# A routed-expert layer on one core: places behind the first two filled with heavy and light experts in turn

## The reference, cut to what matters

```python
logits = x2 @ w_router + b_router            # 256 x 32
top_vals, top_idx = lax.top_k(logits, 4)     # each token goes to 4 of 32 experts
# per expert e, for its tokens:
h = x2[tok] @ w_gu[e] + b_gu[e]              # w_gu[e]: 1024 x 2048, 8.39 MB
y = (clip(u) + 1) * (g * sigmoid(1.702 * g)) # g, u: the halves of h, clamped
out[tok] += gate * (y @ w_down[e] + b_down[e])   # w_down[e]: 1024 x 1024, 4.19 MB
```

## Time and profile before

| | us |
|---|---|
| median of three runs | 1148.16 |
| the profiled execution, its own time | 1148.07 |
| its span in the trace | 1146.2 |
| TensorE busy | 1062.1 |
| DMA queue of the weights, share of 16 engines' span | 91.2% |

### The profile page before, as it was taken

How to read it: one execution, slowest core, us unless ns; L and a number is a source line. 1 busy time by engine, 2 the same in 40 slices (tenths; PEclk the granted TensorE clock), 3 DMA queues, 4 the chain that set the end, 5 groups by cost and what they waited for, 6 DMA issues and landing times.

```text
span 1146.2 us, 20182 instructions
## 1 busy us (share of the span) xinstructions
PE 1062.1 (93%) x8033; PEld 465.3 (41%) x8035; DVE 443.7 (39%) x1311; ACT 153.0 (13%) x333; POOL 61.1 (5%) x39
## 2 busy tenths in 40 slices
PE   9999999998999669999976669999979989999997
PEld 8876559542333223333321113333323323333333
DVE  2767577582433113333321113333313323333324
ACT  2142111220111001111100001111101101111101
POOL 0503370000000000000000000000000000000000
PEclk9999999999999879999988879999989989999999
DMA  9965256989999999999999999999999999999995
GB/s 331 364 234 184 106 193 253 378 322 429 424 433 432 431 432 431 432 432 431 432 431 432 433 430 432 432 431 435 429 432 431 432 431 429 418 431 427 433 425 246
DMA packets 36105, 444.87 MB, mean 388 GB/s; under 512 B 3876, under 2 KB 5160, under 8 KB 21256
## 3 DMA queue, kind: packets, MB, share of 16 engines
q1 hardware_dynamic: 33320, 439.86, 91.2%
q10 hardware_dynamic: 2752, 4.54, 1.4%
HBM read 443.34 MB, written 1.05 MB: 388 GB/s over the span
## 4 chain that ended last, share of the span: by engine, by line
PE 73%; DMA 19%; DVE 3%; another core or an unknown queue 2%; ACT 1%; issue 1%; DVEq 0%; SPq 0%; POOL 0%; POOLq 0%
PE bank L1007 26%; DMA ring<-in_w_gu 14%; PE bank L1032 12%; PE bank L983 6%; PE bank L691 6%; DMA ring<-in_w_down 6%; PE bank L637 5%; PE bank L970 3%; PE bank L816 2%; PE bank L879 2%; PE bank L976 2%; PE bank L1014 1%; PE bank L1020 1%; PE bank L1025 1%; PE bank L1001 1%
## 5 line engine op out<-in xcount | busy, mean ns | idle before, releaser
L1007 PE MATMUL bank<-ring,wk 128*32 128x512 f32 x3072 | 373.3, 637 | 62.8 <-DMA ring<-in_w_gu 62.7
L1007 PEld LDWEIGHTS bank<-ring,wk 128*32 128x32 f32 x3072 | 104.1, 116 | 304.0 <-issue 265.7
L1032 PE MATMUL bank<-ring,wk 128*32 128x512 f32 x1632 | 203.7, 596 | 4.0 <-DMA ring<-in_w_down 4.0
L2025 DVE TENSOR_SCALAR wk<-bank 128x256 f32<-128x256 f32 x51 | 21.6, 424 | 462.1 <-PE bank L1007 462.1
L983 PE MATMUL bank<-wk 64*128 64x512 f32 x416 | 103.3, 615 | 3.3 <-ACT wk L1426 2.9
L1032 PEld LDWEIGHTS bank<-ring,wk 128*32 128x32 f32 x1632 | 63.6, 109 | 71.5 <-issue 42.5
L1414 ACT ACTIVATE wk<-wk 128x256 f32<-128x256 f32 x51 | 21.2, 417 | 458.2 <-DVE wk L2025 458.2
L637 PE MATMUL bank<-ring 128*128 128x256 f32 x320 | 70.7, 381 | 0.0
L691 PE MATMUL bank<-ring 128*128 128x512 f32 x152 | 66.4, 593 | 0.0
L983 PEld LDWEIGHTS bank<-wk 64*128 64x128 f32 x416 | 35.8, 186 | 72.0 <-issue 64.2
L637 PEld LDWEIGHTS bank<-ring 128*128 128x128 f32 x320 | 60.2, 190 | 8.9 <-issue 0.8
(11 more groups left out here) (369 smaller groups left out, 876.4 us busy)
## 6 DMA issues: line engine op xcount, KB each, us to landing
ring<-in_w_gu SPq DMA_DIRECT2D x55, 4096.0 KB, 34.3
ring<-in_w_down SPq DMA_DIRECT2D x27, 4096.0 KB, 38.3
ring<-in_w_gu SPq DMA_DIRECT2D x18, 2048.0 KB, 13.2
ring<-in_w_down SPq DMA_DIRECT2D x9, 2048.0 KB, 11.4
ring<-in_w_in SPq DMA_DIRECT2D x4, 2048.0 KB, 19.1
ring<-in_w_ck SPq DMA_DIRECT2D x2, 2048.0 KB, 21.5
ring<-in_w_cv SPq DMA_DIRECT2D x2, 2048.0 KB, 17.7
ring<-in_w_cq SPq DMA_DIRECT2D x2, 2048.0 KB, 8.5
```

The costliest lines, as they stand in the source:

```text
L1007: ins = mm(hidden(bank, g), rows[:, kk, c, :], half_columns(w[:, kk, :], g), start=False, stop=2 * c + kk == KT - 1, skip_group_check=True)
L1032: ins = mm(strip(7, 2 * d + b), actT[:, b, 2 * c + gg, :], wd[:, gg, b, 512 * d:512 * d + 512], start=c == 0 and gg == 0 and b == 1, stop= ...
```

## The change

Only the table of ranks by place is new. Behind the first two places it takes heavy and light experts in turn: ranks 3, 17, 2, 18, and then 4, 19, 5, 20, and so on to 16, 31.

```diff
-RANK_AT = [0, 1] + [2 + i for i in (21, 11, 10, 12, 16, 3, 23, 5, 18, 8, 19, 26, 13, 27, 6, 7, 9, 4, 25, 15, 1, 24, 22, 0, 20, 14, 2, 17, 29, 28)]
+RANK_AT = [0, 1, 3, 17, 2, 18] + [r for i in range(13) for r in (4 + i, 19 + i)]
 HEAVY_AT = RANK_AT.index(UNROLL)
```

## The result

The changed kernel takes 1197.2 us (median of four runs, 1196.4 to 1198.5), 1.0425 times the time before, with a 95% interval from 1.0412 to 1.0438. The forecast was 1195.5 us. The profiled execution took 1196.87 us, its span is 1195.0 us. Beside the three runs given for the kernel before there was a fourth, a slow one of 1237.53 us, which is left out of the ratio.

The account below looks back on a forecast made before the run. Weight transfers bound the kernel; place 14's load flows from 654.4 us, about 50 us late, plus 524.7 us for eighteen experts, 14.6 us tail and 1.9 us outside the span: 1195.5 us rounded, range 1190 to 1202.

Parts of the forecast that it names:

- The bound: Before the change, weight transfers set the time at 29.15 us an expert; TensorE's idle time costs nothing.
- The shortage: Places 2 to 14: loads wait for the last pass two places before, leaving the queue empty for 50.3 us altogether.
- The start of an empty queue: A load that finds the weight queue empty pays 3.3 us for its start; bounds 0 and 3.8 us.
- My row: Profile row of the fastest such landing, 13.0 us after issue against 9.72 us for its bytes, giving 3.3 us.
- fixed cost of about 2.0 us: The skill's cost for a DMA, which would make the forecast sum 1.3 us smaller than the 3.3 us read.
- the dips around 1010 us: In the kernel before, two dips to 396 and 418 GB/s, said to hold most of the 2.7 us lost late.
- The tail: Time behind the last landing, said to keep its 14.6 us since the last two places hold one pass each.
- The lead: Rival: orders still queued at 305 us hide two more passes at place 2, and time falls to 1145.4 us; chance 2%.
- The stream did not catch up: Rival denied here: the stream regains at some gaps what it lost at others, near no change; chance 2%.
- The low clock: Rival: from place 16 slow-clocked passes make TensorE the bound, four pairs adding 34 us, 1229 us; chance 3%.
- The rule of the Trainium skill: Bound near 358 GB/s: a pair would take 70 us of transfers, so little but the first gap is lost.
- four holes: Empty-queue times summed as 25.2 + 12.8 + 9.2 + 3.1 us, the last at places 10, 12 and 14.

Follow-up runs that it names:

- the single exchange: The kernel before with places 2 and 7 exchanged, so that place 2 has three passes and place 7 one: 1173.49 us, ratio 1.0219.
- The turned pairs: The changed kernel with each heavy-light pair turned round, the light expert first: 1182.94 us, ratio 1.0302 to the kernel before.
- the moved heaviest expert: The changed kernel with the four-pass expert of place 4 and the two-pass expert of place 22 exchanged: 1175.30 us, ratio 1.0234 to the kernel before.

## Why the prediction was right, point by point

**The bound.** The stream was the bound before, at 29.15 us an expert. After, from place 16 on, it is again: the first units of places 16 and 27 start at 722.18 and 1042.71 us, 29.14 us apart on average.

**The shortage.** Place 4's load was put at 334.64 us and went out at 334.96; place 6's at 404.65 and 405.03; place 14's at 651.14 and 651.53. The 0.3 to 0.4 us are the front's, which ended that much later. TensorE ran without a wait for weights up to 721 us, as forecast. That these passes are what sets the time is shown by the kernels with four more matmuls, and that the queue's hole is never made up by the single exchange.

**The start of an empty queue.** I took 3.3 us. From place 14's issue to place 16's first unit the transfers leave 722.18 - 58.3 - 9.72 - 651.53 = 2.6 us. My row stands 0.7 us above this. The Trainium skill's fixed cost of about 2.0 us ("DMA: Bandwidth & Descriptors", "Anatomy of one DMA") stands 0.6 us below; the section gives it for DMAs that GpSimd issues, and these are issued by SyncE.

**The rest.** Place 16's first unit was put at 722.4 us and came at 722.18. That this is so close is in part luck: the start was 0.7 us shorter than I took, and the front's 0.3 to 0.4 us hid half of it. The last landing was put at 1179.1 us and TensorE started on it at 1180.44: 1.3 us of the difference. It comes from one expert that took 30.74 us instead of 29.14, between 1042.71 and 1073.45 us; I had put no such loss behind place 16, though the kernel before lost 2.7 us late. I had laid most of those 2.7 us to the dips around 1010 us, but by their rates (396 and 418 GB/s for 10 us each) the dips make 1.2 us. The whole loss follows from these terms: 651.53 + 2.6 - 604.2 = 49.9 us at place 14, less the 2.7 us that the kernel before lost late, plus the 1.6 us that the changed one lost late, is 48.8 us. The tail is the same 14.6 us, so that the low clock in the light stretch (granted 0.86 between 1000 and 1175 us) did not reach it. Sum 1193.7 + 1.3 = 1195.0 us of span.

**The rivals.** The lead did not cover place 2: 26 GB/s at 313 to 338 us. The stream did not catch up. The low clock slows the first matmuls behind each wait (32 records in 5.60 us at 731.99 us, where half of 7.05 us is their time at the full clock), but behind 722 us TensorE still waits some 104 us in all for weights (busy 354 of the 458 us up to 1180 us), so its passes did not become the bound. The rule of the Trainium skill ("DMA: Bandwidth & Descriptors", "Where 436 GB/s comes from") by which transfers from HBM are bound near 358 GB/s is not borne out by this kernel on one core: 425 to 433 GB/s over stretches of 142 us and more wherever the queue was fed.

**What the point of decision is.** I had described the loss as four holes. The turned pairs and the moved heaviest expert show it better as one account: the passes of TensorE from place 2 to the last shortage, less the transfers in the same stretch. Two passes less at place 4 removed 22 us of it together with all small holes behind it.

## What to carry to other kernels

With a ring of n blocks the fetch for a block waits for the last use of the block n places before. So where the stream is the bound, order uneven blocks so that at no place the compute done since the start exceeds the transfers by more than the lead, and begin with cheap ones; an average under the bound is not enough. The lead can be no larger than the ring, so cheap blocks first do not pay for a row of dear ones at the end: the light experts first gave the slowest order of all, 1223.88 us. Idle time of the bound resource is lost for good, while the order that avoids it is worth nothing further. And look at what a piece of work covers before it is removed: the wait beneath it comes up, and the clock may fall with it.

## What the runs showed of the hardware that I had not expected

In the kernel before without the scatter, a wait of 1.61 us in a pass of 14.8 us was at times followed by the lower clock level (1.2 GHz): the same 15 matmul records took 2.09 us in one pass and 3.26 us in the next, with the same wait in both. Why one pass is hit and the other not is open. The table by stretch of TensorE alone (busy, granted clock, DMA share, GB/s) around the second:

```profile
834.00:836.60 2.60, 0.99 (x11) 1.00 1.14 492
...
838.40:841.70 3.30, 3.30 (x23) 0.64 1.06 457
```

A load of 4.19 MB issued to an empty queue cost 2.6 us beyond the time of its bytes. That is not a delay before the first byte. The same table for the changed kernel, where the load for place 4 is issued at 334.96 us:

```profile
335.00:336.00 1.00, 1.00 (x16) 1.00 0.65 164
336.00:337.00 1.00, 1.00 (x13) 1.00 1.36 360
337.00:338.00 1.00, 1.00 (x12) 1.00 0.30 131
338.00:339.00 1.00, 1.00 (x8) 1.00 0.99 426
```

Bytes move between 335 and 336 us, about a microsecond after the issue, and 426 GB/s are reached from 338 us on. Up to then the bytes moved are 1.5 us short of 431 GB/s; where the other 1.1 us lie is open.

One expert in the last third of the stream took 1.6 us longer than all others, in the changed kernel between 1042.71 and 1073.45 us. The stream moved 430 GB/s between 1042 and 1074 us, hardly under its usual 431, so a slower stream does not explain it. Its cause is open.
